# A hybrid decoder layer on eight cores: two intermediate results are kept token-major in DRAM and transposed where they are loaded, and weight preparation moves to other stages

## The chip, the cores and the metric

One Trainium2 chip. The same program runs on 8 cores; each core handles one of the 8 sequences of the batch, and the cores exchange nothing. The metric is the device time of the slowest core in microseconds (us).

Each core has five instruction streams that run in order: PE (TensorE), ACT (ScalarE), DVE (VectorE), POOL (GpSimd) and SP (SyncE). In this kernel SP issues nearly all plain DMAs and all DMA transposes; POOL issues the weight loads, which convert f32 to bf16 on the way.

## The reference

Per sequence: 4096 tokens, model width 1024. In short:

```python
def mixer_sublayer(h, ...):                      # sub-layer 1
    xn = rms_norm(h, norm_mix)
    qa, ka, va, ra, za, qb, kb, vb = jnp.split(xn @ w_in, IN_OFFSETS, axis=-1)
    log_a = jax.nn.log_sigmoid(za @ w_gla_gate + b_gla_gate) / GLA_TAU
    o_a = gla_chunked(qa * (GLA_DK ** -0.5), ka, va, log_a)     # gated linear attention
    o_a = rms_norm(o_a, gla_out_norm) * jax.nn.silu(ra)
    qd = rope_partial(rms_norm(qb, dil_q_norm), cos, sin)       # 3 groups of 8 heads
    kd = rope_partial(rms_norm(kb, dil_k_norm), cos, sin)
    o_b = dilated_attention(qd, kd, vb)          # windows 128, 512, 2048; dilations 1, 4, 16
    g_a, g_b = jnp.split(jax.nn.sigmoid(xn @ w_merge_gate + b_merge_gate), 2, axis=-1)
    merged = g_a * (o_a @ w_br_gla) + g_b * (o_b @ w_br_dil)
    return h + merged @ w_mix_out

def memory_cross_attention(h, mem, ...):         # sub-layer 2, 256 memory tokens, 4 heads
    xn, mn = rms_norm(h, norm_x), rms_norm(mem, norm_mem)
    q = rms_norm(xn @ w_xq, x_q_norm)
    k, v = jnp.split(mn @ w_xkv, 2, axis=-1)
    k = rms_norm(k, x_k_norm)
    p = softmax(q k^T / 16)
    return h + (p v) @ w_xo

def conv_glu_ffn(h, ...):                        # sub-layer 3, D_FF = 2816
    xn = rms_norm(h, norm_ffn)
    a, u = jnp.split(xn @ w_ffn_up, 2, axis=-1)
    c = b_ffn_conv + causal_conv3(a, w_ffn_conv)
    return h + (gelu(c) * u) @ w_ffn_down
```

## The kernel before

The kernel records every instruction through helpers (`fw.mm`, `fw.act`, `fw.dma`, `fw.dmat` and so on), so that all matmuls carry line L249, all plain DMAs L241 and all DMA transposes (`dmat`) L245. The helper puts an instruction at the end of its engine's stream and makes it wait for whatever last wrote or read its buffers. Nothing reorders afterwards: the order on each engine is the order of the Python code. Buffers lie at fixed SBUF offsets in an arena; a new buffer over an old one waits for the old one's users. A DMA also waits for the one that last used its semaphore, of which SP has 24 and POOL 8, so that POOL never has more than eight DMAs under way.

The program has five stages.

**GLA stage.** The 4096 tokens are 32 chunks `c` of 128, or 8 slices `s_` of 512 (four chunks each). An iteration takes state and output of chunk `c` (`R_o`, `R_on`), the v and r projections of chunk `c+1` (`R_v`, `R_r`), the scaling of a later tile `i` (`nscale`, `ntrans`) and a part of the next slice's q, k and gate projections (`P_qk`, `P_za`, `P_z`, `P_e`). `xn` is the normalised input with features on partitions; tiles of slices 2 to 7 reach it through DRAM: `ntrans` stores the token-major tile `xs` to `xs_d`, and after the fourth tile of a slice eight transposes `xnT<-xs_d` bring in the slice, one for each 128 features (`kc`). `P_za` is the first to read them. Its result `za` is copied out of PSUM by DVE and read by `P_z`. The chunk's gated output `on` (128 tokens by 1024) is transposed in SBUF to `oT` and stored to `oaT_d` (`R_t`).

**Dilated stage.** 96 items (3 groups of 32 blocks of 128 queries). An item projects q, k, v with `wd`, rotates on POOL, transposes `qkb` by DMA, and runs scores, softmax and the product with v. Results go to `og_d`.

**Merge stage.** Eight slices `s_` by eight feature blocks `m`. `merge_br(s_, m, br)` runs the gate projection of one branch (8 matmuls, tile `sig`) and the branch projection (8 matmuls with `oat` for the GLA branch, br 0; 4 with `obt` for the dilated branch, br 1), and multiplies them (`mab`); POOL adds the branches into `mT`. `oat` has one buffer, loaded with four DMAs for each slice. `obt` comes from `og_load`, `og_comb` (POOL adds the three groups), `og_div` (DVE, into `obn`) and `og_trans` (transpose). In the odd blocks `mix(i)` projects a 128-token tile of the previous slice (16 matmuls with `wmo`), adds the residual (`xtT`), stores `h1_d` and leaves the normalised tile `xsT`; `x2trans` transposes that into `x2s` and stores it to `xn2_d` (printed as xn_d). The same stage computes keys and values of the memory (`kv_...`).

**Cross-attention stage.** A loop over steps `k` (32 tiles and 12 steps of drain). A step loads tile `k+2` of `xn2_d` into `x2i`, projects q (`q_proj(k)`, 16 matmuls with `wxq`), normalises it (`q_stats` on ACT, `q_norm` on DVE), transposes it (`qTx`), and for earlier tiles runs scores, denominators and, from step 10, the output product `x_out(k-10)` with the memory product `MX` (values times `w_xo`), the residual `h1x`, the store to `h2_d` and the third norm. `mix` of the last four tiles and `x2trans` of the last five fall in steps 0 to 4. `MX` is built by `kv_mx` in steps 5 to 8. The first 17 of 22 `w_up` slabs (`wup`) are loaded in this loop.

**Feed-forward stage.** Eight slices of 512 tokens: 22 blocks `up`, then the down projection with `wdn`.

`fw.dmat` always issues on SP:

```python
    def dmat(self, out, in_, xr=()):
        o, i = out.ap, in_.ap
        return self._add("sp", lambda e: e.dma_start_transpose(out=o, in_=i), [in_], [out], dma=True, xr=xr)
```

## Time and profile before

| what | value |
|---|---|
| time, median of 3 runs | 3142.36 us (3138.27 to 3156.69) |
| profiled execution: its time | 3135.5 us |
| its span, slowest core (core 3) | 3134.0 us |
| spans of the eight cores | 3121.5 to 3134.0 us |
| granted TensorE clock, mean of the cores | 0.960 to 0.963 |
| busy PE, DVE, ACT, POOL | 90%, 56%, 39%, 32% of the span |
| DMA transposes issued | xnT 48, oT 32, qkT 96, obt 32, x2s 32, qTx 32, x3T 32 |

The span is the time from the first to the last instruction of one core; the execution's own time is 1.5 us longer. PE is busy for most of the span, but not evenly: the share differs by stage, and the granted clock (1.00 is 2.4 GHz, 0.50 is 1.2 GHz) falls after stretches in which PE had little to do. A matmul at the lower clock counts as busy for longer, so a busy share alone hides that loss. The stages lie at about 0 to 565 us (GLA and what comes ahead of it), 565 to 1243 (dilated), 1243 to 1783 (merge), 1783 to 2180 (cross-attention, with its drain) and from there to the end (feed-forward).

### The profile page before, as it was taken

The page shows a single profiled execution, that of the slowest core. Times are in us where ns is not written, and L with a number is a line of the kernel's source. Part 1 is how long each engine was busy: PE and PEld are TensorE (multiplying, and loading weights), DVE is VectorE, ACT ScalarE, POOL GpSimd, SP SyncE. Part 2 cuts the span into 40 slices and gives each one's busy share as a digit, 9 for nine tenths or more (in the row PEclk, how much of TensorE's full clock was granted, in tenths as well). Part 3 has the DMA queues.
Part 4 walks back from the last instruction along what each step waited for, and adds up shares of the span by engine and source line. Part 5 has one row for each costly group of instructions (what it writes and reads, how often), then busy time and mean ns, then how long its engine had stood idle before and what let it go on. Part 6 is the DMA issues. An engine that isn't in the chain of part 4 may idle for free.

```text
span 3134.0 us, 51255 instructions; the slowest of 8 cores (3121.5 to 3134.0 us)
## 1 busy us (share of the span) xinstructions
PE 2821.4 (90%) x15278; PEld 1345.7 (43%) x15278; DVE 1762.7 (56%) x2745; ACT 1223.3 (39%) x2478; POOL 987.5 (32%) x1460
## 2 busy tenths in 40 slices
PE   4878898799999998998988948887999999999998
PEld 2434444355665443443444413332434444444443
DVE  3766676588777885333433324554645645744753
ACT  3455554466555665222222236664412211211211
POOL 1432333577777796233333510000100100100100
PEclk9999999899999999999999979998999999999999
DMA  6443333553563666666777496777641121021110
GB/s 133 103 120 99 96 87 86 98 103 82 92 114 83 132 140 138 154 156 167 199 169 157 120 183 157 187 195 189 138 106 28 41 68 34 35 67 51 31 54 28
DMA packets 384132, 346.42 MB, mean 111 GB/s; under 512 B 292312, under 2 KB 294900, under 8 KB 382452
## 3 DMA queue, kind: packets, MB, share of 16 engines
q1 hardware_dynamic: 367616, 291.58, 35.8%
q0 software_dynamic: 15392, 51.09, 10.7%
q8 instruction: 128, 2.10, 0.3%
q14 instruction: 144, 1.18, 0.1%
q10 hardware_dynamic: 852, 0.47, 0.1%
HBM read 215.96 MB, written 108.92 MB: 104 GB/s over the span
## 4 chain that ended last, share of the span: by engine, by line
PE 66%; DMA 10%; DVE 8%; ACT 6%; issue 5%; SPq 3%; POOL 1%; DVEq 0%; ACTq 0%; POOLq 0%
PE psum L249 66%; SPq L245 3%; DMA x2s_209<-xsT_207 2%; ACT jh L275 1%; DVE on_112 L308 1%; ACT junkX L275 1%; DMA oT_113<-on_112 1%; SPq L241 1%; ACT junkA L275 1%; DMA wdn<-w_dn 1%; DMA x2s_240<-xsT_208 1%; DMA x2i_221<-xn_d 1%; DMA obt_180<-obn_188 1%; DMA cstb<-consts 1%; DMA obt_179<-obn_188 1%
## 5 line engine op out<-in xcount | busy, mean ns | idle before, releaser
L249 PE MATMUL psum<-wd_141,xnT 128*128 128x512 bf16 x768 | 186.3, 388 | 11.8 <-DMA wd_141<-w_dil 11.8
L318 POOL COPY hist<-abt_287 128x2 f32<-128x2 f32 x88 | 18.1, 206 | 562.9 <-ACT abt_287 L317 562.9
L249 PE MATMUL psum<-wd_176,xnT 128*128 128x512 bf16 x768 | 185.8, 385 | 0.2 <-issue 0.2
L249 PE MATMUL psum<-wd_177,xnT 128*128 128x512 bf16 x768 | 182.0, 380 | 0.2 <-issue 0.2
L317 ACT COPY abt_287<-psum 128x512 f32<-128x512 f32 x88 | 50.2, 570 | 245.7 <-PE psum L249 245.7
L275 ACT ACTIVATE gl_286<-cv_1_282 128x512 f32<-128x512 f32 x88 | 55.5, 631 | 217.9 <-DVE cv_1_282 L308 217.9
L275 ACT ACTIVATE gl_285<-cv_0_281 128x512 f32<-128x512 f32 x88 | 55.5, 631 | 213.6 <-DVE cv_0_281 L308 213.5
L282 DVE TENSOR_TENSOR mab_196<-psum,sig_195 128x512 f32<-128x512 f32 x64 | 44.2, 691 | 148.8 <-PE psum L249 140.8
L249 PEld LDWEIGHTS psum<-wd_176,xnT 128*128 128x128 bf16 x768 | 102.9, 147 | 48.4 <-issue 0.3
L249 PEld LDWEIGHTS psum<-wd_141,xnT 128*128 128x128 bf16 x768 | 80.8, 116 | 82.7 <-issue 18.2
L282 DVE TENSOR_TENSOR qg_145<-psum,gqk 128x512 f32<-128x512 f32 x96 | 65.8, 685 | 82.3 <-ACT sq_143 L275 66.8
L282 DVE TENSOR_TENSOR mab_197<-psum,sig_194 128x512 f32<-128x512 f32 x64 | 44.0, 688 | 117.8 <-ACT sig_194 L275 57.0
L275 ACT ACTIVATE sig_195<-psum,gall 128x512 f32<-128x512 f32 x64 | 44.0, 688 | 157.6 <-PE psum L249 157.4
L318 POOL COPY hist<-abt_288 128x2 f32<-128x2 f32 x88 | 17.2, 195 | 280.0 <-ACT abt_288 L317 280.0
L249 PEld LDWEIGHTS psum<-wd_177,xnT 128*128 128x128 bf16 x768 | 67.6, 98 | 75.0 <-issue 0.3
L282 DVE TENSOR_TENSOR qg_146<-psum,gqk 128x512 f32<-128x512 f32 x96 | 65.8, 685 | 59.2 <-ACT sq_143 L275 44.8
L275 ACT ACTIVATE sq_144<-psum 128x512 f32<-128x512 f32 x96 | 57.5, 599 | 87.2 <-PE psum L249 87.2
L300 DVE TENSOR_SCALAR cv_0_281<-abt_287,gall 128x512 f32<-128x512 f32 x88 | 48.1, 546 | 72.2 <-ACT abt_287 L317 72.2
L275 ACT ACTIVATE sq_143<-psum 128x512 f32<-128x512 f32 x96 | 57.4, 598 | 79.9 <-PE psum L249 79.9
L300 DVE TENSOR_SCALAR cv_1_282<-abt_288,gall 128x512 f32<-128x512 f32 x88 | 48.1, 546 | 71.4 <-ACT abt_288 L317 71.4
L282 POOL TENSOR_TENSOR mT_193<-mab_196,mab_197 128x512 bf16<-128x512 f32 x32 | 40.4, 1264 | 142.9 <-DVE mab_196 L282 117.6
L275 ACT ACTIVATE sig_194<-psum,gall 128x512 f32<-128x512 f32 x64 | 43.6, 682 | 105.3 <-PE psum L249 105.2
(760 smaller groups left out, 7492.6 us busy)
## 6 DMA issues: line engine op xcount, KB each, us to landing
ogl_178<-og_d SPq DMA_DIRECT2D x96, 260.0 KB, 4.2
og_d<-og_172 SPq DMA_DIRECT2D x32, 260.0 KB, 2.1
og_d<-og_173 SPq DMA_DIRECT2D x32, 260.0 KB, 2.5
og_d<-og_174 SPq DMA_DIRECT2D x32, 260.0 KB, 2.1
oaT_d<-oT_113 SPq DMA_DIRECT2D x32, 256.0 KB, 2.1
oat<-oaT_d SPq DMA_DIRECT2D x32, 256.0 KB, 3.8
xtT_205<-x SPq DMA_DIRECT2D x16, 512.0 KB, 5.5
h_d<-xtT_205 SPq DMA_DIRECT2D x16, 512.0 KB, 4.9
```

The costliest lines, as they stand in the source:

```text
L241: return self._add(q, lambda e: e.dma_start(out=o, in_=i, **kw), [in_], [out], dma=True, join=join, xr=xr)
L245: return self._add("sp", lambda e: e.dma_start_transpose(out=o, in_=i), [in_], [out], dma=True, xr=xr)
L249: return self._add("pe", lambda e: e.matmul(o, l, r, start=start, stop=stop), [lhsT, rhs], [out], xr=xr)
L275: return self._add("act", lambda e: e.activation(o, i, func, **kw), reads, writes, xr=xr, xw=xw)
L282: return self._add(eng, lambda e: e.tensor_tensor(o, a, b, op), [in0, in1], [out], xr=xr, xw=xw)
L300: return self._add(eng, lambda e: e.tensor_scalar(o, a, s1, s2, op0, **kw), reads, writes)
L308: return self._add(eng, lambda e: e.scalar_tensor_tensor(o, a, scalar, b, op0, op1), reads, [out])
L317: return self._add("act", lambda e: e.copy(o, i), [in_], [out])
L318: return self._add(eng, lambda e: e.tensor_copy(o, i), [in_], [out])
```

## The change

- `oaT_d` becomes `oa_d` (tokens by features). `R_t` stores `on` as it is, `on` has two buffers, `oT` is gone; `oat_load` transposes while loading, four DMA transposes for each slice.
- `xn2_d` is token-major as well: `x2store` stores `xsT`, `x2load` transposes while loading. `x2s` is gone.
- GLA: the tile scaled in an iteration is `c+9`, no longer `c+8`, and the eight transposes of a slice come four after the third chunk of a slice and four after the fourth.
- The dilated weights are two half tiles; the first half of the first group starts loading at chunk 23.
- Merge: in block 7 branch 0 comes first, then `oat_load`, then branch 1. The steps `og_comb`, `og_div`, `og_trans` run two blocks earlier than before.
- `w_xo` is loaded and `MX` built in the merge stage (slices 5 and 6); `w_xq` is four tiles; the first three `x2load` stand in slice 7.
- Cross-attention: `x2load(k+2)` stands between `q_norm` and the transpose of q; `loadh` is issued by POOL, one step earlier; `up_load` runs as half slabs from step 0 to 27, and whole slabs from step 32; `wup`, `x3T` and `h2f` have other offsets.

The core of the diff (offset tables and allocations left out):

```diff
     def R_t(c):
-        oT = oTr.next()
-        fw.dmat(oT[:, :, :], cst_[c]["on"][:, :])
-        fw.dma(V(oaT_d[c], oaT_d[c].t[c]).rearrange("p (c t) -> p c t", c=8), oT[:, :, :])
+        fw.dma(V(oa_d[c], oa_d[c].t[c * 128:(c + 1) * 128, :]), cst_[c]["on"][:, :])
...
-        i = c + 8
+        i = c + 9
...
+        if nx or s_ == 0:
+            if c4 == 2:
+                xtrans(s_ + 2, range(4)) if s_ + 2 < NS else None
+            elif c4 == 3:
+                xtrans(s_ + 2, range(4, 8)) if s_ + 2 < NS else None
...
+        if c == 23:
+            wd_alloc(0, 0)
         if c == 27:
             c_early()
-        if c > 27:
-            bg(2)
+        if c >= 23:
+            bg()
...
     def oat_load(s_):
         for t_ in range(4):
-            b = oaT_d[s_ * 4 + t_]
-            fw.dma(ogc["oat"][:, t_, :, :].rearrange("p c t -> p (c t)"), V(b, b.t[s_ * 4 + t_]), join=True)
+            b = oa_d[s_ * 4 + t_]
+            fw.dmat(ogc["oats"][t_][:, :, :], V(b, b.t[rows(s_ * 4 + t_), :]))
...
-    def x2trans(i):
-        x2 = x2r.next()
-        fw.dmat(x2[:, :, :], TA[i]["xs"][:, :])
-        fw.dma(V(xn2_d[i], xn2_d[i].t[i]), x2[:, :, :].rearrange("p c t -> p (c t)"))
+    def x2store(i):
+        fw.dma(V(xn2_d[i], xn2_d[i].t[rows(i), :]), TA[i]["xs"][:, :])
...
+    def x2load(i):
+        TC[i]["x2"] = ogc["x2i"].next()
+        fw.dmat(TC[i]["x2"][:, :, :], V(xn2_d[i], xn2_d[i].t[rows(i), :]))
...
             if (s_, m) >= (0, 3):
-                merge_br(s_, m, 1)
-                merge_br(s_, m, 0)
-            if m == 7 and s_ + 1 < NS:
-                oat_load(s_ + 1)
+                if m < 7:
+                    merge_br(s_, m, 1, False)
+                    merge_br(s_, m, 0, True)
+                else:
+                    merge_br(s_, m, 0, False)
+                    if s_ + 1 < NS:
+                        oat_load(s_ + 1)
+                    merge_br(s_, m, 1, True)
...
-            if 0 < s_ < NS - 1:
-                i = (s_ + 1) * 4 + m // 2
...
+            if L % 2 == 0 and 8 <= (L + 10) // 2 < NT:
+                og_comb((L + 10) // 2)
+            if L % 2 == 0 and 8 <= (L + 8) // 2 < NT:
+                og_trans((L + 8) // 2)
+            if L % 2 == 1 and 8 <= (L + 9) // 2 < NT:
+                i = (L + 9) // 2
+                og_div(i)
...
     for k in range(NT + 12):
-        bg(2)
-        if 5 <= k < 9:
-            kv_mx(k - 5)
...
-            x2trans(NT - 5 + k)
+            x2store(NT - 5 + k)
...
-        if k + 2 < NT:
-            x2load(k + 2)
-        if 0 <= k - 9 < NT:
-            loadh(k - 9)
+        if 0 <= k - 8 < NT:
+            loadh(k - 8)
+        if k < 28:
+            up_load(k // 2, k % 2)
...
             q_norm(k)
+            if 3 <= k + 2 < NT:
+                x2load(k + 2)
             q_trans(k)
...
-        if 6 <= k < 19:
-            up_load(k - 6)
...
-        if NT + 1 <= k < NT + 5:
-            up_load(13 + k - NT - 1)
+        if NT <= k < NT + 5:
+            up_load(14 + k - NT)
```

What this makes of the order is shown at three places. First SP in the GLA stage, about one slice, before (`xt` are input tiles, `xsA` scaled tiles):

```order
L241 DMA xs_d<-xsA_67 128x1024
L245 DMA_TRANSPOSE oT_113<-on_112 128x8x128
L241 DMA oaT_d<-oT_113 128x1024
L241 DMA xt_61<-x 128x1024
L241 DMA xs_d<-xsA_68 128x1024
L245 DMA_TRANSPOSE xnT<-xs_d 128x512 x8
L245 DMA_TRANSPOSE oT_113<-on_112 128x8x128
L241 DMA oaT_d<-oT_113 128x1024
```

and now:

```order
L241 DMA xs_d<-xsA_68 128x1024
L245 DMA_TRANSPOSE xnT<-xs_d 128x512 x4
L241 DMA oa_d<-on_112 128x1024
L241 DMA xt_62<-x 128x1024
L241 DMA xs_d<-xsA_67 128x1024
L245 DMA_TRANSPOSE xnT<-xs_d 128x512 x4
L241 DMA oa_d<-on_113 128x1024
```

The eight transposes stood in one row ahead of the transpose that frees the only `on`; now four stand a chunk earlier, and `on` leaves by a plain store.

Second, SP in the merge stage from block 6 of slice 1 to the start of slice 2 (`ogl` holds the dilated results, `h_d` is `h1_d`), before:

```order
L245 DMA_TRANSPOSE x2s_209<-xsT_207 128x8x128
L241 DMA xn_d<-x2s_209 128x1024
L241 DMA oat<-oaT_d 128x1024 x4
L241 DMA ogl_178<-og_d 128x520 x3
L241 DMA h_d<-xtT_206 128x1024
L245 DMA_TRANSPOSE obt_179<-obn_188 128x4x128
L241 DMA xtT_205<-x 128x1024
```

and now:

```order
L245 DMA_TRANSPOSE obt_182<-obn_191 128x4x128
L241 DMA xtT_209<-x 128x1024
L241 DMA xn_d<-xsT_210 128x1024
L245 DMA_TRANSPOSE oat<-oa_d 128x8x128 x4
L241 DMA ogl_181<-og_d 128x520 x3
L241 DMA h_d<-xtT_209 128x1024
L245 DMA_TRANSPOSE obt_183<-obn_191 128x4x128
```

The last `obt` transpose of a slice stood behind the `oat` loads and now stands ahead of them; the `oat` loads have become transposes, and the transposes of `xsT` have left.

Third, POOL in the cross-attention stage; before, behind the last `mix`:

```order
L282 TENSOR_TENSOR nssT_184<-nssT_184,mhalf 128x1
L241 DMA wup_263<-w_up 128x2048
L241 DMA wup_264<-w_up 128x2048
L241 DMA wup_265<-w_up 128x2048
L241 DMA wup_266<-w_up 128x2048
L241 DMA wup_267<-w_up 128x2048
```

and now, from the same place:

```order
L282 TENSOR_TENSOR nssT_187<-nssT_187,mhalf 128x1
L241 DMA wup_251<-w_up 128x1024
L241 DMA wup_252<-w_up 128x1024 x2
L241 DMA wup_273<-w_up 128x1024 x2
L241 DMA h1x_246<-h_d 128x1024
L241 DMA wup_274<-w_up 128x1024
L241 DMA h1x_247<-h_d 128x1024
L241 DMA wup_274<-w_up 128x1024
```

Thirteen whole slabs stood in one row with nothing between; now half slabs alternate with the loads of `h1x`, which SP issued before.

## Rows read from the trace of the kernel before

**Rows 1.** Stages: length, busy PE, PEld, DVE, ACT, POOL; granted clock, DMA share, GB/s

```profile
140.00:565.00 425.00, 365.32 (x1897) 177.92 (x1894) 289.89 (x531) 225.28 (x515) 150.69 (x171) 0.93 0.38 99
...
1243.00:1790.00 547.00, 498.99 (x2308) 226.50 (x2308) 191.52 (x270) 124.39 (x205) 199.07 (x202) 0.96 0.66 159
1790.00:1913.00 123.00, 72.19 (x276) 28.75 (x277) 29.62 (x51) 47.16 (x142) 13.64 (x27) 0.78 0.88 173
1913.00:2122.00 209.00, 181.98 (x830) 79.63 (x829) 120.63 (x175) 134.01 (x383) 0.00 (x0) 1.00 0.72 185
```

**Rows 2.** PE's waits, 140 to 565 us: waiter, releaser, total, times, longest

```profile
PE psum L249 <- DVE za_70 L318: 15.0, 3, 5.2
PE psum L249 <- DVE za_69 L318: 15.0, 3, 5.5
PE psum L249 <- DMA xnT<-xs_d: 11.4, 14, 2.3
```

**Rows 3.** Timeline of one slice's hand-over in the GLA stage; brackets: idle before, releaser

```profile
340.18 11.52 SPq L245 DMA_TRANSPOSE xnT<-xs_d  x8
...
355.12 2.25 DVE L308 SCALAR_TENSOR_TENSOR on_112<-psum,hs_115,G_139 128x256 bf16<-128x256 f32 x4 [8.23 <-DMA oT_113<-on_112]
...
359.60 1.86 PE L249 MATMUL psum<-za_70,wgg 16*128 16x512 bf16 x4 [4.90 <-DVE za_70 L318]
```

**Rows 4.** Busy time in the same place

```profile
350.00:360.00 10.00, 1.94 (x5) 0.41 (x6) 3.80 (x7) 0.00 (x0) 1.10 (x1) 0.63 0.66 165
360.00:373.00 13.00, 13.00 (x59) 6.24 (x58) 5.55 (x12) 11.49 (x24) 3.38 (x6) 0.76 0.29 84
```

**Rows 5.** PE's waits, 560 to 600 us

```profile
PE psum L249 <- DMA wd_141<-w_dil: 11.8, 1, 11.8
```

**Rows 6.** PE's waits, 1243 to 1790 us

```profile
PE psum L249 <- DMA obt_179<-obn_188: 21.4, 3, 9.2
PE psum L249 <- DMA obt_180<-obn_188: 20.3, 3, 10.5
```

**Rows 7.** Busy time right behind one of these waits

```profile
1420.00:1436.00 16.00, 16.00 (x66) 6.84 (x65) 5.15 (x7) 2.07 (x3) 5.05 (x4) 0.86 0.11 32
```

**Rows 8.** Feed-forward: four x3T transposes alone; then five plain 512 KB transfers

```profile
2399.00:2407.00 8.00, 8.00 (x39) 3.63 (x37) 5.62 (x9) 1.74 (x3) 0.74 (x3) 1.00 0.69 133
...
2552.00:2564.00 12.00, 12.00 (x57) 5.41 (x56) 7.34 (x11) 3.58 (x7) 1.52 (x6) 1.00 0.60 220
```

**Rows 9.** PE's waits, 1790 to 1913 us

```profile
PE psum L249 <- DMA x2i_222<-xn_d: 23.5, 1, 23.5
PE psum L249 <- DMA x2i_220<-xn_d: 9.0, 1, 9.0
```

**Rows 10.** Timeline of PE: mix of step 0, q_proj of step 8, first matmul of step 9

```profile
1783.01 3.62 PE L249 MATMUL psum<-wmo,mT_204 128*128 128x512 bf16 x16
...
1897.76 3.62 PE L249 MATMUL psum<-wxq,x2i_222 128*128 128x512 bf16 x16
...
1905.03 0.59 PE L249 MATMUL psum<-ptsx_232,cstb 128*128 128x512 bf16 x2 [2.79 <-ACT ptsx_232 L275]
```

**Rows 11.** Busy time while the first eight slabs load; timeline of SP there

```profile
1831.00:1866.00 35.00, 8.21 (x28) 3.18 (x29) 4.62 (x9) 6.26 (x21) 4.77 (x9) 0.64 1.00 189
...
1832.55 4.58 SPq L245 DMA_TRANSPOSE x2s_209<-xsT_207  x1
1860.73 0.32 SPq L241 DMA_DIRECT2D xn_d<-x2s_209  x1
```

**Rows 12.** The chain that ended last, two steps of the cross-attention loop

```profile
1933.47 1.27 DVE xsX_256 L308
...
1943.15 1.27 DVE xsX_257 L308
```

**Rows 13.** PE's waits, 2122 to 2300 us

```profile
PE psum L249 <- DMA qTx_231<-qn_1_228: 7.4, 1, 7.4
...
PE psum L249 <- DMA wdn<-w_dn: 6.1, 2, 4.1
```

More of the change, by code:

```diff
@@ L916, in build @@
     nstat(8)
+    nscale(8)
+    ntrans(8)
+    nload(11)
+    nstat(9)
     R_r(0)
@@ L1113, in og_alloc @@
         ogc["oat"] = ar.at("oat", (128, 4, 8, 128), BF16, 112 * K_)
+        ogc["oats"] = [ogc["oat"].sub("oat", ogc["oat"].t[:, t_]) for t_ in range(4)]
     def og_load(i):
@@ L1170, in merge_br, with mb_y @@
         fw.act(sg[:, :], pg[:, :], AF.Sigmoid, bias=bmg[:, br * 8 + m:br * 8 + m + 1])
+        T1["g%d" % br] = sg
+    def mb_y(s_, m, br, last):
+        sl = slabs[m]
         py = P.next()
@@ L1173, in merge_br @@
             for kc in range(8):
-                fw.mm(py[:, :], sl[:, kc, :], ogc["oat"][:, :, kc, :], start=(kc == 0), stop=(kc == 7))
+                ap = ogc["oat"].t[:, :, kc, :]
+                ob = [V(b, ap) for b in ogc["oats"]]
+                fw.mm(py[:, :], sl[:, kc, :], ob[0], start=(kc == 0), stop=(kc == 7), xr=ob[1:])
         else:
@@ L1376, in kv_mx, with ar_ring, x2i_alloc @@
                 fw.copy("act", KV["MX"][h][:, mb, cs_], p_[:, :])
+    TC = [dict() for _ in range(NT)]
+    def ar_ring(name, k, shape, dt, off):
+        n = Arena.nbytes(shape, dt)
+        return Rot([ar.at("%s%d" % (name, i), shape, dt, off + i * n) for i in range(k)])
+    def x2load(i):
+        TC[i]["x2"] = ogc["x2i"].next()
+        fw.dmat(TC[i]["x2"][:, :, :], V(xn2_d[i], xn2_d[i].t[rows(i), :]))
+    def x2i_alloc():
+        ogc["x2i"] = ar_ring("x2i", 3, (128, 8, 128), BF16, 188 * K_)
@@ L1430, in build, with up_load @@
     gfb = rx.sb("gffb", (128, 1024), F32)
+    KV["gq"] = rx.sb("gqx", (128, 256), F32)
+    fw.dma(KV["gq"][:, :], dram_bc(SM["x_q_norm"], 256))
     h1r = Reg(ar, 48 * K_, 64 * K_).ring("h1x", 4, (128, 1024), F32)
[L1433 to L1435 removed]
     WUP = [None] * NFC
[L1438 to L1442 removed]
+    UP_OFF = [32 + 4 * i for i in range(4)] + [150 + 4 * i for i in range(9)] + [199, 12, 24, 28, 188, 192, 0, 4, 8]
+    def up_load(fc, hf=None):
+        if not hf:
+            WUP[fc] = ar.at("wup%d" % fc, (128, 8, 2, 128), BF16, UP_OFF[fc] * K_)
+        c_ = slice(0, 2048) if hf is None else slice(hf * 1024, hf * 1024 + 1024)
+        fw.dma(WUP[fc][:, :, :, :].rearrange("p c j n -> p (c j n)")[:, c_], V(WD["w_up"], WD["w_up"].t[fc][:, c_]), q="pool",
+               join=bool(hf))
     F_ = {}
     XL = {}
[L1446 removed]
     def t1b_late():
@@ L1460, in build @@
     PB = P
-    TC = [dict() for _ in range(NT)]
     def q_proj(i):
@@ L1669, in build @@
                 UPD.append(cur)
-    for fc in range(17, NFC):
+    for fc in range(19, NFC):
         BG.append(lambda fc=fc: up_load(fc))
```

146 lines of the change are left out of this document (66 added, 80 removed).

## The prediction

> **What bounds the kernel now.** I first read the busy time by stage [rows 1]. The reader is to see that PE is the engine that matters, and that its lost time lies in three stages. In the GLA stage 425 - 365 = 60 us are idle and the granted clock is 0.93; in the merge stage 48 us are idle at 0.96; at the start of cross-attention 51 of 123 us are idle at 0.78. A clock below 1.00 is a second loss: the same matmuls take longer and still count as busy. The rest of cross-attention (1913 to 2122) is different: PE is busy for 182 of 209 us at full clock, and the chain repeats one DVE instruction every 9.68 us [rows 12]; it runs through ACT's statistics and DVE's normalisation, so the step length is a loop of those two engines. The change leaves that loop as it is.
>
> Then I read PE's waits stage by stage. GLA: 30.0 us for `za` and 11.4 for `xnT` [rows 2], in six hand-overs from slice to slice. The timeline shows how they hang together [rows 3]: eight transposes keep SP's queue busy for 11.5 us; behind them stands the transpose of the only `on`; DVE waits 8.2 us for `on`; the copy of `za` stands behind that on DVE; and PE waits for the copy. PE works 1.9 us in 10, and in the next 13 the clock is 0.76 [rows 4]. Merge: 41.7 us for `obt` [rows 6], six waits at the start of a slice, and behind such a wait the clock is 0.86 for 16 us [rows 7]. Start of cross-attention: 32.5 us in two waits for `x2i` alone [rows 9].
>
> **The change part by part.** All terms are against the profiled execution, 3135.5 us.
>
> *GLA hand-over.* With four transposes one chunk earlier and a plain store of a second `on`, no step of rows 3 is left in which DVE waits for a transpose. What is late next is the copy of `za` itself, which DVE reaches after the four `on` products and two products for the r gate; PE needs it one matmul group after the last of them. I put that at 1.1 us for each hand-over. So 41.4 / 6 = 6.9 us of waiting become 1.1, a gain of 5.8. The clock gives 13 x 0.24 = 3.1 us more [rows 4]. Six hand-overs: 6 x 8.9 = **-54 us**. Bounds: -35 (waits only, no clock) to -66 (nothing waits). The 32 transposes of `on` are moved to the merge stage and priced there; the two extra instructions of the prologue only come earlier and cost nothing.
>
> *Dilated start.* PE waits 11.8 us for the last part of `wd` [rows 5]. Half of the load now starts four chunks earlier, but the last piece is still issued at chunk 30. Only contention falls: **-5 us**, bounds 0 to -12.
>
> *Merge.* `obt` is ready two blocks earlier, against a wait that is at most 10.5 us, while a block has at least 28 matmuls of 0.22 us [the pace of rows 10: 3.6 us for 16]. That removes 41.7 us [rows 6] and the low clock behind it: 16 x 0.14 = 2.2 us and some 0.6 in the wait, for five of the waits, 14 us. Added is first `kv_mx`: 32 matmuls x 0.22 = 7 us that came before in a stage where PE was idle. Added is also a new wait: `oat` is now four transposes issued when branch 0 of block 7 is done and needed when branch 0 of the next slice begins. Between lie 12 + 16 + 12 + 8 matmuls, 48 x 0.22 = 10.4 us (6.9 after slice 0, where there is no `mix`). Four transposes of this form took 8 us with nothing beside them [rows 8]. In this stage the DMA share is 0.66 [rows 1], so I stretch 8 to 12 us: 1.6 us at six slices and 5 at one, with a little clock **12 us**. Bounds 0 and 88: if each of the four held SP for 4.6 us, as one does under slab loads [rows 11], and the last landed 4.6 us later, 23 - 10.4 = 12.6 us at seven slices; I stay near rows 8 because no slabs load here. Queued on SP behind the wait for branch 0 are `ogl`, the `h1` store and the next `obt`, all with a block to spare now. Sum: -41.7 - 14 + 7 + 12 = **-37 us**, bounds -49 to +39.
>
> *Start of cross-attention.* Steps 0 to 8 last from 1783.0 to 1905.0, 122 us [rows 10]. The last of them, undisturbed, took 7.3 us, from its q projection to the next step. With `kv_mx` gone and `x2i` loaded two steps ahead from tiles stored long before, four steps with `mix` (32 matmuls, 6.9 us of PE, say 7.2) and five of 7.6 (with the denominators ahead of q) make 67 us. What could still delay them are the slabs: eight at once filled the DMA engines for 35 us, and one transpose took 28.2 us from issue to the store behind it [rows 11]. Now the same stretch brings eight half slabs and four `h1x` tiles, about half the bytes; half of 28 is 14 us, against the 15 us by which `x2i` is ahead. The scores wait for q with less lead, so I charge 15 us. 122 - 82 = **-40 us**, bounds -20 (35 us of delay) to -55 (none).
>
> *The steps behind it.* Each of 32 steps swaps a plain 256 KB load for a transpose, and 28 carry half a slab. Five plain 512 KB transfers took 12 x 0.60 = 7.2 us of all DMA engines, 0.72 per 256 KB; four transposes 8 x 0.69 = 5.5, 1.4 each [rows 8]. That is 0.7 us more. A slab is at most 35 / 8 = 4.4 us [rows 11], less for what ran beside it, say 3.2; half is 1.6. Of a 9.68 us step that is 24%, on a share of 0.72: 0.96. Near full, but each load has two steps of lead, and `h1x` too. **+8 us**, bounds 0 and +45 (28 x 1.6: no half slab is hidden).
>
> A rule can be weighed here. The trace has a transpose at twice the time of a plain load of the same bytes [rows 8]. The Trainium skill (Advanced Engine Details and Errata, section X-Bar Transpose (TRN2)) says that transposing DMAs on this chip are as fast as regular ones. By that rule the swap would be free, and the +8 would be about +5; the trace disagrees, 1.4 against 0.72 us.
>
> *End of cross-attention and feed-forward.* Four slabs in one burst delay q once by 7.4 us, and `wdn` is 6.1 us late [rows 13]. The burst is now five slabs separated by `h1x` loads: **-6 us**, bounds 0 to -14. `wdn` starts two blocks of 16 matmuls earlier, 7 us, and covers the wait: **-6 us**, bounds 0 to -9.
>
> *Sum.* -54 - 5 - 37 - 40 + 8 - 6 - 6 = -140: 2995.5 for an execution like the profiled one, which ran 6.9 us below the median of the three runs. Predicted median: **3002 us**, 4.5% faster.
>
> **The rivals.** *More comes back.* All waits go, and the clock stays at 1.00: the bounds of GLA, merge and cross start together give -39 more, 2963. For it speaks that all of these waits have a named cause that is moved; against it, that DMA traffic gets denser.
>
> *The DMA engines become the bound of cross-attention.* At 0.96 of estimated load a step may no longer fit; +45 instead of +8 and only -20 at the start: 3059. For it: share 1.00 and 28 us for a transpose under slabs [rows 11]. Against: the slabs are thinned out.
>
> *`oat` takes the place of `obt`.* 12.6 us at seven slices, 88 instead of 12: 3078. Against: rows 8.
>
> *GLA does not get what it should.* If DVE, busy for 290 of 425 us [rows 1], is what really paces the hand-over, the copy of `za` stays late, half of 54 is lost: 3029.
>
> *Slower.* SP is one in-order queue, and when the DMA engines are full it is held while issuing a transpose (4.6 us for one in rows 11). A cross-attention step now issues two. If each stands until the slabs ahead have drained, as the 28 us of rows 11, a step would grow with every half slab. It decides from about 140 / 28 = 5 us more per step, 14.7 in place of 9.68; with 7 us it gives 3002 + 28 x 7 = 3198. Against: between 1913 and 2122 the share was 0.72 and the loop never waited for a transpose.
>
> **How the numbers follow.** Forecast, 2980 to 3025: 0.50. More comes back (2940 to 2980): 0.17. GLA half: 0.10. DMA bound: 0.11. `oat`: 0.06. Slower: 0.03. Two of the shortfalls together, 3085 to 3140: 0.03. A measurement of this kernel can tell about 1% (31 us) from no change. Faster by more needs under 3111: 0.50 + 0.17 + 0.10 + 0.11 + 0.06 and half of the last, 0.95. Within 1%: 0.02; slower: 0.03. The range leaves out the best few per cent and the last three cases: 2948 to 3070.
>
> **What would show it.** In the profile after: no `za` wait above 2 us and no DVE wait for a transpose in GLA, clock near 1.00 there; no `obt` wait, `oat` waits of a few us at slice starts; steps 0 to 9 of cross-attention in 80 us with `x2i` waits under 15 us together; steps of 9.7 us after that at a DMA share near 0.95. The prediction is wrong if these steps lengthen, if `oat` waits exceed 5 us at each slice, or if GLA hand-overs still show PE idle for 5 us.

## The result and the profile after

The changed kernel takes 2985.78 us (median of 4 executions, 2980.53 to 2987.35); the kernel before, run beside it, 3149.53 us. The ratio is 0.9476, with a 95% interval of 0.9431 to 0.952. The profiled execution took 2980.53 us, with a span of 2979.0 us on core 2 and a granted clock of 0.982 to 0.985. Where one die of an execution ran at a lower clock than the other, here and below only its undisturbed die is read, and its time is left out.

First, busy time by stage in the profile after, with the columns of [rows 1].

```profile
140.00:500.00 360.00, 337.12 (x1826) 167.83 (x1827) 275.90 (x505) 216.11 (x494) 140.84 (x156) 0.99 0.33 92
1180.00:1673.00 493.00, 490.48 (x2317) 225.61 (x2314) 188.53 (x266) 132.62 (x219) 199.35 (x202) 1.00 0.68 165
1673.00:1766.00 93.00, 59.93 (x230) 23.65 (x230) 29.15 (x51) 35.97 (x115) 12.90 (x26) 0.82 0.82 168
1766.00:1975.00 209.00, 183.44 (x836) 80.38 (x836) 118.12 (x171) 134.92 (x390) 19.08 (x36) 1.00 0.97 202
```

In GLA 23 of 360 us of PE are idle (60 of 425 before), in the merge 2.5 of 493, at a clock of 0.99 and 1.00 against 0.93 and 0.96. The start of cross-attention is still poor: 33 of 93 us idle, clock 0.82. Behind it the DMA share went from 0.72 to 0.97, while PE does the same work in the same time.

To see where the time went, the span is cut at five instructions of PE that exist in both kernels. These are their rows in the timeline of core 2 after (for the down projection no row is shown; the view of the second ends amid its 16 matmuls); two of them answer to [rows 10].

```profile
1144.96 1.89 PE L249 MATMUL psum<-xnT,slab_193 128*128 128x512 bf16 x8
...
1673.25 2.96 PE L249 MATMUL psum<-wmo,mT_207 128*128 128x512 bf16 x13 [1.01 <-DVE xtT_209 L282]
...
1766.53 0.59 PE L249 MATMUL psum<-ptsx_241,cstb 128*128 128x512 bf16 x2 [2.33 <-ACT ptsx_241 L275]
...
2030.78 5.49 PE L249 MATMUL psum<-x3T,wup_250 128*128 128x512 bf16 x16 [10.66 <-DMA x3T<-x_d]
```

Read in this way on every core, the stages last as follows (us, mean of the cores; "tail" is from the first matmul with `wdn` to the end). The column "out" counts the half slabs of `w_up` that POOL has issued before PE reaches step 9 (a whole slab counts as two); it is the same on every core. All twelve runs of the next section stand here too.

| kernel | GLA and dilated | merge | steps 0 to 8 | out | step 9 to first up | up, first slice | tail |
|---|---|---|---|---|---|---|---|
| before | 1203.2 | 576.7 | 123.2 | 26 | 270.4 | 96.9 | 856.9 |
| changed | 1147.6 | 529.3 | 93.9 | 12 | 259.0 | 100.8 | 845.3 |
| gla_row8 | 1150.1 | 528.5 | 91.5 | 12 | 256.5 | 99.5 | 844.8 |
| gla_spread_only | 1162.4 | 575.9 | 121.5 | 26 | 270.4 | 97.2 | 856.0 |
| oat_late (die 0) | 1146.5 | 540.2 | 90.6 | 12 | 254.2 | 98.8 | 846.2 |
| obt_late | 1146.5 | 582.9 | 92.6 | 12 | 256.2 | 98.3 | 845.0 |
| slabs_late | 1147.8 | 529.3 | 78.3 | 4 | 273.0 | 98.2 | 844.2 |
| x3_early | 1148.1 | 529.2 | 91.2 | 12 | 254.3 | 97.3 | 846.4 |
| loadh_sp | 1149.2 | 529.2 | 109.7 | 28 | 263.7 | 98.4 | 843.8 |
| before_thin | 1201.2 | 576.9 | 125.6 | 26 | 270.9 | 98.0 | 849.6 |
| half10_x3 (die 0) | 1148.2 | 527.2 | 76.6 | 2 | 258.6 | 98.6 | 845.3 |
| half6_x3 | 1147.6 | 530.4 | 82.7 | 6 | 258.2 | 97.3 | 845.2 |
| whole2_x3 | 1147.3 | 529.0 | 75.2 | 2 | 256.9 | 99.4 | 844.2 |
| x3_steps | 1147.1 | 528.5 | 75.7 | 2 | 253.9 | 99.8 | 845.2 |

So the change brings 55.6, 47.4, 29.3, 11.4, -3.9 and 11.6 us, 151.5 in all before rounding. The time itself is that of the slowest core, which is why single cores matter below. Columns that a kernel does not touch repeat within some 5 us; between the cores of one execution the merge of the kernel before spreads more widely, 568 to 585 us.

The waits show the same. PE in the GLA stage after (120 to 500 us), which answers to [rows 2], and the copy and use of `za` at one hand-over:

```profile
PE psum L249 <- DVE on_113 L308: 13.5, 17, 2.6
PE psum L249 <- DVE za_69 L318: 4.4, 3, 2.3
...
PE psum L249 <- DVE za_70 L318: 3.1, 3, 1.0
```

```profile
272.68 0.67 DVE L318 CAST za_69<-psum 16x512 bf16<-16x512 f32 x1
327.91 0.68 DVE L318 CAST za_70<-psum 16x512 bf16<-16x512 f32 x1
...
328.84 1.02 PE L249 MATMUL psum<-za_70,wgg 16*128 16x512 bf16 x4 [1.04 <-DVE za_70 L318]
```

`za` fell from 30.0 to 7.5 us and the `xnT` wait is gone. DVE waits for no transpose any more, on any core, where it waited 42.2 us for `oT` on core 3 before. What is left is PE's wait for `on`, 15.4 us, which was there before (11.6). Behind this stage the wait for `wd` [rows 5] went from 11.8 to 5.9 us. One slice takes 327.91 - 272.68 = 55.2 us. In the merge there is no `obt` wait any more [rows 6], and `oat` costs little (1.8 us here, at most 6.4 on any core). This is PE's wait in the merge, and these are its longest at the start of cross-attention (1670 to 1768 us), which answer to [rows 9]:

```profile
PE psum L249 <- DMA oat<-oa_d: 1.8, 1, 1.8
```

```profile
PE psum L249 <- DMA x2i_230<-xn_d: 7.4, 1, 7.4
PE psum L249 <- DMA qTx_239<-qn_0_236: 6.9, 1, 6.9
PE psum L249 <- DMA x2i_228<-xn_d: 5.9, 2, 3.6
```

The timeline of SP there answers to [rows 11]. The second of these waits is for a transpose of q that goes out at 1713.17 us and lands 22.0 us after its issue; the transpose of `x2i` behind it holds the queue for 15.47 us.

```profile
1713.17 3.62 SPq L245 DMA_TRANSPOSE qTx_239<-qn_0_236  x1
...
1717.56 15.47 SPq L245 DMA_TRANSPOSE x2i_228<-xn_d  x1
```

What they stand behind is in the timeline of POOL:

```profile
1709.78 1.14 POOL L241 DMA_DIRECT2D wup_252<-w_up  x2
1710.90 1.08 POOL L241 DMA_DIRECT2D wup_273<-w_up  x2
...
1727.45 0.53 POOL L241 DMA_DIRECT2D wup_275<-w_up  x1 [1.57 <-DMA wup_273<-w_up]
1785.48 0.53 POOL L241 DMA_DIRECT2D h1x_246<-h_d  x1 [57.50 <-DVE h1x_247 L282]
1786.04 0.53 POOL L241 DMA_DIRECT2D wup_276<-w_up  x1
```

The half slabs are spread over the steps in the program, but not in time. Behind the last `mix` POOL waits for nothing but landings until the four buffers of `h1x` are used up. From 1709.18 to 1727.45 us it issues the half slabs of steps 3 to 11 and four `h1x` loads, the first eight of these transfers within 4 us, while PE is at steps 4 and 5. Then it stands 57.5 us for a buffer of `h1x`, and from there it issues one half slab for each step, behind an `h1x` load. So the burst of the kernel before is smaller, not gone: on every core twelve half slabs are out before step 9.

The loop behind step 9 is untouched, [rows 12]: 9.68 us from step to step, at a DMA share of 1.06 (shares count the time of packets, and can pass 1).

```profile
1801.95 0.59 PE L249 MATMUL psum<-ptsx_242,cstb 128*128 128x512 bf16 x2 [1.32 <-ACT ptsx_242 L275]
1811.63 0.59 PE L249 MATMUL psum<-ptsx_243,cstb 128*128 128x512 bf16 x2 [1.32 <-ACT ptsx_243 L275]
```

```profile
1800.00:1850.00 50.00, 42.44 (x193) 18.32 (x191) 28.43 (x42) 32.61 (x94) 5.29 (x10) 1.00 1.06 220
...
2020.00:2040.00 20.00, 9.34 (x36) 3.79 (x36) 4.67 (x6) 3.46 (x7) 2.11 (x6) 0.74 1.20 184
```

The last row is new and bad: at the end of cross-attention PE is busy for 9 of 20 us. SP's timeline tells why. The four transposes of `x3T` are issued among the five whole slabs, and hold SP for 29.37 us; PE waits 10.7 us for them. The `qTx` and `wdn` waits of [rows 13] are gone.

```profile
1999.23 29.37 SPq L245 DMA_TRANSPOSE x3T<-x_d  x4
```

Five of the eight cores have this `x3T` wait, 3.5 to 12.4 us.

### The profile page after: what moved, and what is told of

The parts are those of the page before. It is cut to its first block, busy times and chain, and to the rows that moved or that the text cites. A ratio compares the mean times of both kernels' runs of the same rounds, so it can differ in the third digit from the quotient of the medians.

```text
span 2979.0 us, 51194 instructions; the slowest of 8 cores (2971.9 to 2979.0 us)
## 1 busy us (share of the span) xinstructions
PE 2782.5 (93%) x15278; PEld 1337.4 (45%) x15278; DVE 1760.0 (59%) x2745; ACT 1228.2 (41%) x2484; POOL 1011.8 (34%) x1502
## 4 chain that ended last, share of the span: by engine, by line
PE 75%; DVE 9%; ACT 5%; issue 5%; DMA 3%; SPq 1%; POOL 1%; DVEq 0%; ACTq 0%; POOLq 0%
PE psum L249 74%; ACT jh L275 1%; SPq L245 1%; ACT junkX L275 1%; DMA x2i_228<-xn_d 1%; DVE on_113 L308 1%; DMA cstb<-consts 1%; DVE on_112 L308 1%; ACT junkA L275 1%; DVE qn_0_236 L308 0%; PE psum L253 0%; DMA wvr_138<-w_gvr 0%; DMA wvr_59<-w_gvr 0%; DVE qn_1_237 L308 0%; DVE qn_2_238 L308 0%
## 5 line engine op out<-in xcount | busy, mean ns | idle before, releaser
L282 DVE TENSOR_TENSOR qg_146<-psum,gqk 128x512 f32<-128x512 f32 x96 | 65.8, 686 | 76.7 <-ACT sq_144 L275 55.2
L249 PE MATMUL psum<-wd_1_142,xnT 128*128 128x512 bf16 x384 | 99.7, 382 | 5.9 <-DMA wd_1_142<-w_dil 5.9
L249 PE MATMUL psum<-wd_0_177,xnT 128*128 128x512 bf16 x384 | 103.4, 392 | 0.0
L249 PE MATMUL psum<-wd_0_141,xnT 128*128 128x512 bf16 x384 | 101.1, 386 | 0.5 <-DVE G_140 L308 0.5
L249 PE MATMUL psum<-wd_0_179,xnT 128*128 128x512 bf16 x384 | 99.2, 381 | 0.0
L249 PE MATMUL psum<-wd_1_178,xnT 128*128 128x512 bf16 x384 | 98.5, 379 | 0.0
L249 PE MATMUL psum<-wd_1_180,xnT 128*128 128x512 bf16 x384 | 98.5, 379 | 0.0
L282 DVE TENSOR_TENSOR mab_199<-psum,sig_198 128x512 f32<-128x512 f32 x56 | 38.7, 691 | 100.1 <-PE psum L249 100.1
L275 ACT ACTIVATE sq_145<-psum 128x512 f32<-128x512 f32 x96 | 57.5, 599 | 85.4 <-PE psum L249 85.4
L275 ACT ACTIVATE sig_198<-psum,gall 128x512 f32<-128x512 f32 x64 | 44.0, 688 | 113.1 <-PE psum L249 110.3
L282 POOL TENSOR_TENSOR ogl_181<-ogl_181 128x520 f32<-128x520 f32 x64 | 84.1, 1314 | 7.3 <-DMA ogl_181<-og_d 2.6
L282 DVE TENSOR_TENSOR mab_200<-psum,sig_197 128x512 f32<-128x512 f32 x56 | 38.4, 686 | 70.1 <-ACT sig_197 L275 53.5
```

The costliest lines, as they stand in the source:

```text
L249: return self._add("pe", lambda e: e.matmul(o, l, r, start=start, stop=stop), [lhsT, rhs], [out], xr=xr)
L275: return self._add("act", lambda e: e.activation(o, i, func, **kw), reads, writes, xr=xr, xw=xw)
L282: return self._add(eng, lambda e: e.tensor_tensor(o, a, b, op), [in0, in1], [out], xr=xr, xw=xw)
```

## Experiments

Theory: the hand-over in GLA was slow because the transpose of the one `on` stood behind eight others; the lead in blocks took `obt` away; the half slabs are what still delays the start of cross-attention, and the burst of slabs what delays `x3T`. The rivals stand with each run.

### GLA: which half of the change does it

gla_row8 puts the eight transposes back in one row:

```diff
-            if c4 == 2:
-                xtrans(s_ + 2, range(4)) if s_ + 2 < NS else None
-            elif c4 == 3:
-                xtrans(s_ + 2, range(4, 8)) if s_ + 2 < NS else None
+            if c4 == 3:
+                xtrans(s_ + 2, range(8)) if s_ + 2 < NS else None
```

> The changed kernel, but all eight transposes of xnT stand in one row again, at the last chunk of a slice; the plain store of a second on is kept. Theory A (the transpose of the only on, queued behind the eight, made the hand-over slow): DVE and za stay free of waits, the slice period stays at 55 to 57 us (55.2 changed, 64.9 before), only waits of PE for xnT come back, some 10 us in all; the time is within 15 us of the changed kernel's. Rival B (the row of eight by itself holds the hand-over): the period is back at 62 or more, the GLA stage 40 us longer or more.

gla_spread_only is the kernel before with that half of the change alone (the plain store of `on` left out):

```diff
-        i = c + 8
+        i = c + 9
...
+            if c4 == 2:
+                xtrans(s_ + 2, range(4)) if s_ + 2 < NS else None
+            elif c4 == 3:
+                xtrans(s_ + 2, range(4, 8)) if s_ + 2 < NS else None
```

> The kernel before with one part of the change alone: normalisation one chunk earlier and four transposes of xnT at each of two chunks; on is still a single tile that is transposed by DMA and then stored. Theory A: the wait of DVE for on stays (its transpose stands behind four others now, not eight), so the slice period falls by a part only, from 64.9 to 59 to 62 us, 20 to 35 us faster than before in all. Rival B (the row of eight is the cause): period near 55, 55 to 65 us faster than before. Rival C (spreading alone gives nothing, a transpose of on now waits at two chunks): period 64 or more.

gla_row8 took 2980.96 us, ratio 0.9519 (0.9502 to 0.9536), no more than the changed kernel; gla_spread_only 3090.57 us, ratio 0.9865 (0.9846 to 0.9884). The slice period is read from the copies of `za`, second to sixth, over four: (484.79 - 229.87) / 4 = 63.7 us before, 56.7 with the spread alone, 56.0 with the plain store alone, 55.3 with both. PE's waits in gla_row8, 120 to 500 us, core 2:

```profile
PE psum L249 <- DVE za L318: 7.6, 6, 2.4
...
PE psum L249 <- DMA xnT<-xs_d: 3.8, 5, 1.3
```

DVE's waits in gla_spread_only, core 0, same stretch:

```profile
DVE on L308 <- DMA oT<-on: 3.3, 4, 2.6
```

With the plain store alone the period is what theory A foretold (55 to 57). With the spread alone it is below theory A's 59 to 62 and above rival B's 55. So the slow hand-over needs both links, the row of eight and the transpose of `on` behind it: behind four transposes the wait for `oT` is 2.6 us at most, where it was 8.2 behind eight [rows 3], and eight transposes with no `on` among them cost PE 3.8 us. Either half alone brings over four fifths of the 8.4 us per slice, and the two together little more. Both runs also normalise one chunk earlier, and no run has that alone. In the kernel before, SP stood 1.9 us (338.29 to 340.18) in front of the row until the last `xs` was stored; that is what it can take out of the queue, but its full worth is not shown. My expectation for the spread alone, 20 to 35 us, was too low: 41 in the first column.

### Merge: obt's lead, and the landing of oat

obt_late puts the combining, dividing and transposing back to the old blocks:

```diff
-            if L % 2 == 0 and 8 <= (L + 10) // 2 < NT:
-                og_comb((L + 10) // 2)
-            if L % 2 == 0 and 8 <= (L + 8) // 2 < NT:
-                og_trans((L + 8) // 2)
...
+            if 0 < s_ < NS - 1:
+                i = (s_ + 1) * 4 + m // 2
+                if m % 2 == 0:
+                    og_comb(i)
+                    if m > 0:
+                        og_trans(i - 1)
```

> The changed kernel, with the combining, dividing and transposing of the dilated output at the blocks where the kernel before had them (transposed one block before the slice that reads it), all else as changed. Theory (the lead in blocks is what removed the obt waits): six waits of PE for obt of 5 to 8 us come back, 30 to 45 us, and 10 to 15 us by the clock behind them: 40 to 60 us slower than the changed kernel. Rival (the waits came from what else stood in SP's queue, four loads of oat and a transpose and a store per token tile, and are gone with those or are hidden by branch 0 now standing first in block 7): less than 15 us slower.

Measured: 3031.88 and 3033.22 us; the merge 582.9 against 529.3, 53.6 us longer. PE's waits in the merge, core 1, and the busy time there:

```profile
PE psum L249 <- DMA obt<-obn: 44.1, 6, 10.9
...
PE psum L249 <- DMA oat<-oa_d: 1.4, 1, 1.4
```

```profile
1250.00:1735.00 485.00, 439.98 (x2038) 199.99 (x2036) 173.09 (x241) 117.88 (x198) 177.67 (x181) 0.95 0.60 149
```

The theory holds with its sizes: six waits, 44 us, and the rest, some 10 us, by the clock, which is back at 0.95. The edit also puts the last transpose of a slice behind the `oat` loads again, but that costs little: at the slice start of 1431 us `obn` is ready at 1422.58, its transpose goes out at 1424.85, and PE waits 6.4 us. So it is mostly the lead, and not the place in SP's queue.

oat_late lets the `oat` transposes go out later:

```diff
-                if m < 7:
-                    merge_br(s_, m, 1, False)
-                    merge_br(s_, m, 0, True)
-                else:
-                    merge_br(s_, m, 0, False)
-                    if s_ + 1 < NS:
-                        oat_load(s_ + 1)
-                    merge_br(s_, m, 1, True)
+                merge_br(s_, m, 1, False)
+                merge_br(s_, m, 0, True)
+                if m == 7 and s_ + 1 < NS:
+                    oat_load(s_ + 1)
```

> The changed kernel, with block 7 of a merge slice in the order of the other blocks (branch 1, then branch 0) and the four transposes of oat issued behind it: the matmuls that stand between the end of branch 0 and the next slice's branch 0 fall from 48 to 12 + 8 + 8 and the mix, 6 to 8 us less cover. Theory (landing takes the 12 us that the prediction charged): a wait of 3 to 6 us at each of seven slice starts, with the clock behind it 25 to 50 us in all. Rival (they land in the 8 us of four transposes with nothing beside them): 0 to 2 us each, 0 to 15 us in all.

Measured: ratio 0.9553 (0.953 to 0.9576), 2992.03 and 2994.11 us; the merge 11 us longer. PE's waits there, core 0:

```profile
PE psum L249 <- DMA oat<-oa_d: 12.3, 6, 4.7
```

Some 2 us for each slice, 12 in all, and 5.4 to 17.2 on the four cores: nearer the rival's 0 to 15 than the theory's 25 to 50. (The cover falls from 48 to 36 matmuls, some 2.6 us, not by the 6 to 8 of my expectation.) At the six slice starts where core 0 waits, PE goes on 8.4 to 10.5 us after the first of the four was issued; that is near the 8 us of [rows 8], and below the 12 that the prediction charged.

### Start of cross-attention: slabs, order on SP

before_thin has the half slabs alone, in the kernel before (the new argument of `up_load` is left out):

```diff
...
-        if 6 <= k < 19:
-            up_load(k - 6)
+        if 6 <= k < 32:
+            up_load((k - 6) // 2, k % 2)
```

> The kernel before with one part of the change alone: the thirteen whole up slabs at steps 6 to 18 become 26 half slabs at steps 6 to 31; everything else of the start of cross-attention (transpose, store and load of x2 in one chain, the memory product there) as before. Theory A (the eight slabs that arrive at once are what delays x2i): steps 0 to 9 fall from 124 us to 95 to 105 on the mean of the cores. Rival B (the chain of transpose, store and load on SP delays x2i without them): 115 or more. In both the steps behind stay at 9.68 us, and the end changes by less than 6 us.

3133.8 us, ratio 0.9994 (0.9984 to 1.0004): nothing. Steps 0 to 8 take 125.6 us, 123.2 before, and PE still waits for `x2i`. These are a wait of PE on core 1, and the loads of half slabs by POOL on that core:

```profile
PE psum L249 <- DMA x2i<-xn_d: 31.2, 3, 22.5
```

```profile
L241 POOL DMA_DIRECT2D wup<-w_up x26: 527/535/827, 1836.6 to 1881.4; - x26
```

By its number this is rival B, but the edit did not do what it was made for. With no `h1x` load on POOL's queue the half slabs have little to wait for but landings: all 26 go out within 45 us, and on core 1 of the kernel before the thirteen whole ones do so within 40 (1828.12 to 1868.07). The burst was not thinned out, so whether it or the chain of transpose, store and load delayed `x2i` in the kernel before is not shown.

slabs_late has no slab at the first ten steps of the changed kernel, and doubles the rate later:

```diff
-        if k < 28:
-            up_load(k // 2, k % 2)
+        if 10 <= k < 24:
+            up_load(k - 10)
```

> The changed kernel, with fourteen whole up slabs at steps 10 to 23 of cross-attention, where it has 28 half slabs at steps 0 to 27: no slab at all beside the first ten steps. Theory A (the half slabs delay the transposes of x2i and q at the start): steps 0 to 9 take 75 to 85 us on the mean of the cores (95 changed, 124 before), 10 to 20 us faster if nothing is paid later. Rival B (two transposes a step, the stores and the loads of h1x hold SP by themselves): 90 to 97 us, no gain. Rival C (the loop of ACT and DVE is near the DMA bound: share 1.06 with half a slab a step): with a whole slab a step the 14 steps lengthen from 9.68 by 1 to 3 us each, 14 to 40 us slower behind step 9.

2986.29 us, ratio 0.9537 (0.9515 to 0.956). POOL still runs ahead, and two whole slabs go out before step 9, the equal of four half slabs in place of twelve. Steps 0 to 8 take 78.3 us, 16 less: theory A. But rival C is right too, on some cores: from step 9 to the first up matmul four cores take 253 to 264 us, the other four 284 to 294. Core 7 is one of these; its waits behind step 9, then its SP queue:

```profile
PE psum L249 <- DMA x2i<-xn_d: 33.0, 5, 15.9
PE psum L249 <- ACT ptsx L275: 26.3, 19, 3.6
```

```profile
1837.15 19.83 SPq L245 DMA_TRANSPOSE x2i<-xn_d  x1
...
1892.02 15.42 SPq L245 DMA_TRANSPOSE qTx<-qn  x1
```

Core 2, with the same instructions, kept its 9.68 us at a share of 1.06. Here are the same 50 us on core 7 and on core 2:

```profile
1850.00:1900.00 50.00, 35.98 (x146) 14.71 (x143) 20.31 (x30) 23.66 (x68) 4.22 (x8) 0.88 1.11 164
...
1850.00:1900.00 50.00, 43.41 (x199) 18.93 (x197) 27.73 (x40) 32.56 (x97) 4.24 (x8) 1.00 1.06 242
```

The core that fell behind has the fuller DMA engines and moves fewer bytes, 164 against 242 GB/s. Why one core falls behind and another does not stays open.

loadh_sp sends the `h1x` loads through SP again:

```diff
-        fw.dma(TC[i]["h"][:, :], V(h1_d[i], h1_d[i].t[rows(i), :]), q="pool")
+        fw.dma(TC[i]["h"][:, :], V(h1_d[i], h1_d[i].t[rows(i), :]))
```

> The changed kernel, with the loads of h1x back on the SP queue (a step earlier than in the kernel before, as changed), slabs alone on the POOL queue. Theory A (bytes decide, not the queue): within 5 us of the changed kernel. Rival B (SP is the scarce queue, held 5 to 15 us at a time by transposes): h1x comes late, steps 8 to 14 of cross-attention are 10 to 30 us longer. Rival C (the POOL queue is what makes h1x late, it stood in a burst of nine transfers): 3 to 8 us faster at the start of cross-attention.

3006.89 us in one execution; steps 0 to 8 take 109.7 us, 15.8 more, the loop behind them 4.7 more. `h1x` itself is not late, as rival B had it; on core 5 PE waits for `x2i`. But here too the edit did more than it says, as POOL's loads on that core show:

```profile
PE psum L249 <- DMA x2i<-xn_d: 42.9, 5, 15.8
```

```profile
L241 POOL DMA_DIRECT2D wup<-w_up x28: 527/528/1043, 1687.5 to 1768.3; - x28
```

Without the `h1x` loads among them, all 28 half slabs go out before step 9, in 81 us, where the changed kernel sends twelve and then one for each step. So the bytes at the start are not the same, and the run does not tell a scarce SP queue from a burst of slabs. Across the runs the time of steps 0 to 8 goes with the slabs that are out: 75 to 77 us with two half slabs, 78 with four, 83 with six, 91 to 94 with twelve, 110 with these 28. That is 1.2 to 1.8 us for each beyond two, and leaves nothing that SP's queue would have to explain here. By the same price (an estimate) the 24 further half slabs of the kernel before are 29 to 43 of the 47 us by which its steps are longer, and `kv_mx` another 7: the burst could be nearly all of it.

### End of cross-attention, and a better version

x3_early loads `x3T` at step 20:

```diff
-        if k == NT + 1:
+        if k == 20:
```

> The changed kernel, with the four transposes that load x3T for the feed-forward issued at step 20 of cross-attention, not one step behind the last, where five slabs go out at the same time. Theory A (the slabs hold those transposes, and the first up matmul waits 10.7 us for them, with the clock at 0.74 to 0.91 behind it): the first up matmul comes 8 to 12 us earlier on the cores that waited, the stage behind it loses 4 to 6 us, 10 to 17 us in all on the slowest core. Rival B (another transfer of the same burst becomes the late one, h1x or the wait of yT): 0 to 4 us. Rival C (four transposes amid the loop delay x2i there): up to 10 us slower.

Ratio 0.9507 (0.9477 to 0.9538), 2971.79, 2981.0 and 2985.83 us. The wait is gone on every core (253 to 258 us to the first up matmul, 97 behind it), 8 us on the mean of the cores and 8.7 on the slowest of the profile; the times show little of it.

half10_x3 and half6_x3 add the half slabs from step 10 and from step 6 (`10 <= k < 38`, `6 <= k < 34`); whole2_x3 has whole ones at even steps from 10 to 36:

```diff
-        if k < 28:
-            up_load(k // 2, k % 2)
+        if 10 <= k < 38:
+            up_load((k - 10) // 2, (k - 10) % 2)
...
-        if k == NT + 1:
+        if k == 20:
```

> The changed kernel, with the 28 half slabs at steps 10 to 37 in place of 0 to 27, and x3T loaded at step 20. Theory A (half slabs cost the start of cross-attention 17 us and the loop nothing; the late x3T costs 6 us of steps and 4 us behind them on the mean of the cores): steps 0 to 9 in 77 to 80 us, from there to the first up matmul 253 to 256, then 97: 25 to 30 us below the changed kernel on the mean of the cores, 2950 to 2960 us. Rival B (a half slab a step, when it is beside the slabs of the end, delays the transposes as the whole ones did at steps 10 to 23): 8 to 20 us of that are lost behind step 32, or some cores have x2i waits of 20 us or more in the loop.

> As the other, with the half slabs at steps 6 to 33, so that steps 0 to 4, which also load x, store h1 and store x2, are free of them and steps 6 to 9 are not. Theory A (the half slabs cost only where those other transfers run): 77 to 82 us for steps 0 to 9, the same time in all as with a start at step 10, within 4 us. Rival B (each half slab costs the start alike, some 1.7 us a step for ten steps): 84 to 88 us, 6 to 8 us slower than with a start at step 10.

> As the first, with a whole slab at every second step from 10 to 36 in place of a half slab at every step: the same bytes in the same steps. Theory A (the mean load decides whether the loop keeps its 9.68 us): within 4 us of the halves on every core. Rival B (the size of one burst decides, a whole slab holds the transposes behind it): x2i or q waits in the loop, 10 to 40 us longer on some cores, as with a whole slab at every step (283 to 294 us on four cores, 253 to 264 on the others).

Ratios 0.9481 (0.9467 to 0.9495), 0.9494 (0.948 to 0.9508) and 0.9481 (0.9448 to 0.9514). Steps 0 to 8: 76.6, 82.7 and 75.2 us. half6_x3 is 6 us longer there than half10_x3, as rival B had it (6 to 8), with a time between the two forecasts. Whole slabs at the same mean rate are no worse than halves, so that at this rate the size of one transfer makes no difference that these runs show. But in all three a core or more still loses 6 to 21 us behind step 9, the slowest core gains little, and the times are 2961 to 2987 us. The timeline of SP on core 0 of half10_x3 (274 us where the other three of its die take 253) shows where it begins:

```profile
1867.17 13.52 SPq L245 DMA_TRANSPOSE x3T<-x_d  x4
1889.14 4.95 SPq L245 DMA_TRANSPOSE qTx<-qn  x1
...
1905.11 8.87 SPq L245 DMA_TRANSPOSE x2i<-xn_d  x1
```

On the cores read in these three runs no step from 9 to 22 is longer than 10.5 us, and `x3T` goes out while PE is at step 21. (x3_early has the same row of four beside half slabs and loses at most 5 us on a core, so it does not always cost this much.) x3_steps takes that away: `x3T` goes out one transpose at a step, as those of `x2i` run out, and the whole slabs two steps later.

```diff
-        if k < 28:
-            up_load(k // 2, k % 2)
+        if 10 <= k < 38:
+            up_load((k - 10) // 2, (k - 10) % 2)
...
+        if NT - 3 <= k < NT + 1:
+            x3_load(0, (k - NT + 3,))
+        if NT + 2 <= k < NT + 7:
+            up_load(12 + k - NT)
```

> The changed kernel, with the half slabs at steps 10 to 37, the four transposes of x3T one by one at steps 29 to 32, where the transposes of x2i run out, and the five whole slabs of the end two steps later. Theory A (a core falls behind in the loop where four transposes in a row meet the half slabs, with the SP queue held 10 to 15 us there): no core has waits for x2i or qTx above 3 us behind step 9; 77 us for steps 0 to 9, 253 to 256 from there to the first up matmul, 97 to 100 behind it on every core; the slowest core 2950 to 2965 us, 20 to 30 below the changed kernel. Rival B (any half slab beside the two transposes of a step can set a core back, x3T or not): one or two cores in eight lose 10 to 20 us in the loop as with x3T at step 20, and the time is 2970 to 2980.

2959.14 to 2963.72 us in four executions, ratio 0.9441 (0.942 to 0.9462): below both kernels. All eight cores take 253 to 257 us behind step 9; the waits of the slowest, core 3, from there on:

```profile
PE psum L249 <- ACT ptsx L275: 34.3, 23, 5.9
PE psum L249 <- DVE yT L282: 9.3, 5, 3.6
```

No DMA is left among them, and on the other cores none is longer than 2.1 us: theory A. The run moves `x3T` and the whole slabs, and which of the two moves did it is not separated. Its ratio and that of the changed kernel have overlapping intervals, since the runs of the kernel before beside the changed kernel spread more (3138 to 3163 us; 3131 to 3145 here). The times do not overlap (2959 to 2964; 2981 to 2987), and the stages add up to 26 us less.

## Why the prediction was right

The forecast was 3002 us, 140 less than before plus 6.9; measured were 2985.78, and 151.5 less on the mean of the cores. That the sum is nearer than its terms is partly luck: the merge brought 10 us more than forecast, the start of cross-attention 11 less. By its terms:

- **GLA hand-over and dilated start**, -59 together: 55.6 measured. By the periods it is 63.7 - 55.3 = 8.4 us per slice where the term had 8.9 per hand-over. The reading of rows 3 was right: cut either of the two links in SP's queue and most of it goes (gla_row8, gla_spread_only). The new `za` wait, put at 1.1 us, is 7.5 / 6 = 1.25 on the mean. At the dilated start the wait for `wd` fell by 5.9 us, where 5 were forecast.
- **Merge**, -37: 47.4. `obt` and its clock were right to some 2 us (55.7; obt_late 53.6). The mis-sized part is "12 us" for `oat`: 1.8 us on the profiled core, at most 6.4 on any. The four transposes land as in rows 8, and stretching them from 8 to 12 us for the DMA share of 0.66 was too much (oat_late).
- **Start of cross-attention**, -40: 29.3. The step that failed is the 67 us for the steps without delay. With two half slabs ahead of step 9 they still take 75 to 77 (whole2_x3, x3_steps, half10_x3): q is not ready when the scores need it, and the loop of ACT shows from step 6. In slabs_late these are PE's waits there, core 2:

```profile
PE psum L249 <- DVE qn L308: 6.3, 4, 3.4
PE psum L249 <- DMA qTx<-qn: 6.2, 1, 6.2
PE psum L249 <- ACT ptsx L275: 5.6, 3, 2.3
```

  The 15 us charged for slabs was near: twelve half slabs in place of two cost 93.9 - 76 = 18. But the prediction took the order on POOL for the order in time; it counted eight half slabs, and POOL sends twelve, nine of them in 18 us. It also put the delay of `x2i` down to slabs and chain together, and no run here parts them.
- **Steps behind it**, +8: nothing. The share was estimated at 0.96 and is 0.97, and the steps stayed at 9.68 us; there was no need to charge for nearness to 1. What paces the half slabs there, one for each buffer of `h1x` that comes free, is not in the prediction. On the Trainium skill's rule (Advanced Engine Details and Errata, section X-Bar Transpose (TRN2)) that a transposing DMA is as fast as a plain one, my estimate of the share would be 0.7 / 9.68 = 0.07 lower, 0.89. The measured 0.97 is nearer the estimate without the rule, but that also holds an estimated 1.6 us for a half slab; the measurement that speaks against the rule is rows 8.
- **End of cross-attention**, -6: the `qTx` wait is gone and, as I had not seen, a wait of 6.1 us for `h1x` too, which gives 16 us (x3_early against before). Of this the unforeseen `x3T` wait takes 5 back, and 4 in the next stage: 11.4 and -3.9 us of gain where 6 and nothing were forecast. It is the rival of SP held by transposes, at one place and for 11 us. The `h1x` wait of the kernel before stands in its waits of PE from 2122 to 2300 us:

```profile
PE psum L249 <- DVE h1x_237 L282: 6.1, 1, 6.1
```

- **wdn**, -6: 11.6. The cover was right; the low clock behind the wait (0.97 over 100 us before, 1.00 after) was left out.

Of the two rivals that rest on DMA load, neither came: at half a slab a step the loop holds. slabs_late shows how near they were, since twice that rate puts four of eight cores 30 us behind, by the mechanism that the "slower" rival names.
